# Ten of the gate and up chunks loaded in three transfers: 112, 8 and 8 partitions

## The reference

```
x = x + W_o( g_A * branch_A + g_B * branch_B + g_X * branch_X )   # gated conv, conformer conv, 4-head cross-attention
x = x + MoE(RMSNorm(x))                                          # top 4 of 32 experts
y = RMSNorm(x)
```

```
gu = xe @ w_gu[e] + b_gu[e];  gt, up = split(gu)
act = min(gt, 7) * sigmoid(1.702 * min(gt, 7)) * (clip(up, -7, 7) + 1)
out = act @ w_dn[e] + b_dn[e]      # weighted by the router's softmax gate and summed per token
```

## Time and profile before

| | |
|---|---|
| median of 3 runs | 1346.47 us (1346.32 to 1348.5) |
| the profiled execution | 1352.6 us |
| its span | 1350.5 us |
| TensorE busy | 1261.7 us, 93% |
| VectorE busy | 606.1 us, 45% |
| ScalarE busy | 207.5 us, 15% |
| GpSimd busy | 153.7 us, 11% |
| moved by DMA | 466.74 MB, mean 346 GB/s |

### The profile page before, as it was taken

One profiled execution on the slowest core, in us unless ns is written; L12 is line 12 of the kernel. 1 busy time (PEld: TensorE's weight loads), 2 busy tenths in 40 slices (PEclk: granted clock), 3 DMA queues, 4 the chain that ended last, 5 costly groups with the idle time before them and its releaser, 6 DMA issues.

```text
span 1350.5 us, 18280 instructions
## 1 busy us (share of the span) xinstructions
PE 1261.7 (93%) x7708; PEld 524.7 (39%) x7708; DVE 606.1 (45%) x1013; ACT 207.5 (15%) x305; POOL 153.7 (11%) x177
## 2 busy tenths in 40 slices
PE   7999999999999989999999999999997878787885
PEld 5756766666553222233323332333322222222221
DVE  2898322311345563434434344535444444343445
ACT  4111433210311010001000000101000111000002
POOL 2110100000012120101111111102111121111000
PEclk9999999999989999999999999999999999999898
DMA  9714716464669999999999999999999999999993
GB/s 330 261 63 135 226 63 146 167 249 161 248 261 410 424 424 426 420 428 424 423 425 394 424 407 424 423 425 420 426 421 424 424 423 424 421 424 423 422 425 141
DMA packets 91229, 466.74 MB, mean 346 GB/s; under 512 B 41952, under 2 KB 44540, under 8 KB 66263
## 3 DMA queue, kind: packets, MB, share of 16 engines
q1 hardware_dynamic: 83489, 456.74, 83.3%
q0 software_dynamic: 6240, 5.37, 1.2%
q10 hardware_dynamic: 1374, 2.76, 0.6%
HBM read 472.06 MB, written 4.26 MB: 353 GB/s over the span
## 4 chain that ended last, share of the span: by engine, by line
PE 74%; DMA 23%; DVE 2%; issue 1%; SPq 0%; ACT 0%; DVEq 0%
PE PS L1757 26%; PE PS L1379 16%; PE PS L1787 14%; DMA ring<-in_w_gu 8%; DMA arena<-in_w_gu 8%; PE PS L1819 6%; DMA ring<-in_w_dn 5%; PE PS L1559 4%; DMA arena<-in_w_dn 3%; PE PS L1603 3%; PE PS L1415 2%; PE PS L1319 1%; PE PS L1646 1%; PE PS L1506 0%; DVE XX L1275 0%
## 5 line engine op out<-in xcount | busy, mean ns | idle before, releaser
L1757 PE MATMUL PS<-ring,arena 128*32 128x512 f32 x3408 | 388.8, 605 | 37.1 <-DMA ring<-in_w_gu 19.9
L1757 PEld LDWEIGHTS PS<-ring,arena 128*32 128x32 f32 x3408 | 108.4, 111 | 308.6 <-issue 300.4
L1379 PE MATMUL PS<-arena,ring 128*128 128x320 f32 x768 | 215.2, 436 | 0.1
L1787 PE MATMUL PS<-ring,arena 128*64 128x512 f32 x880 | 198.2, 600 | 14.3 <-DMA ring<-in_w_dn 14.3
L525 POOL DMA_INDIRECT arena<-h_rows,arena x120 | 129.9, 1083 | 710.6 <-DVE arena L1202 645.5
L1379 PEld LDWEIGHTS PS<-arena,ring 128*128 128x128 f32 x768 | 145.0, 191 | 59.6 <-issue 3.2
L1236 DVE TENSOR_TENSOR arena<-PS,XX 128x1024 f32<-128x1024 f32 x32 | 39.2, 1225 | 251.5 <-PE PS L1757 203.9
L795 ACT ACTIVATE arena<-arena 128x1024 f32<-128x1024 f32 x32 | 33.8, 1058 | 716.0 <-DVE arena L1241 716.0
L1757 PE MATMUL PS<-arena 128*32 128x512 f32 x1136 | 128.7, 594 | 8.6 <-DMA arena<-in_w_gu 6.5
L1787 PEld LDWEIGHTS PS<-ring,arena 128*64 128x64 f32 x880 | 62.2, 137 | 148.6 <-issue 148.5
L1172 DVE TENSOR_TENSOR XX<-PS,XX 128x1024 f32<-128x1024 f32 x32 | 39.2, 1224 | 155.5 <-PE PS L1819 155.5
(11 more groups left out here) (210 smaller groups left out, 754.3 us busy)
## 6 DMA issues: line engine op xcount, KB each, us to landing
ring<-in_w_gu SPq DMA_DIRECT2D x96, 2048.0 KB, 25.7
ring<-in_w_dn SPq DMA_DIRECT2D x46, 2048.0 KB, 24.4
arena<-in_w_gu SPq DMA_DIRECT2D x31, 2048.0 KB, 27.5
arena<-in_w_dn SPq DMA_DIRECT2D x17, 2048.0 KB, 30.4
ring<-in_w_in SPq DMA_DIRECT2D x11, 2048.0 KB, 11.1
ring<-in_w_mem_kv SPq DMA_DIRECT2D x2, 2048.0 KB, 20.9
ring<-in_cache_mem_k SPq DMA_DIRECT2D x32, 128.0 KB, 3.3
ring<-in_cache_mem_v SPq DMA_DIRECT2D x4, 1024.0 KB, 6.2
```

What stands on the lines that cost most here:

```text
L1379: last = mm(PS[:, j % 2, 0:T], w[:, k, m * P:(m + 1) * P], hT[:, k, :], start=k == 0, stop=k == KT - 1)
L1757: last = mm(PS[32 * q:32 * q + 32, 2 * i + b, :].rearrange("p (g n) -> p g n", g=2), xT[:, k, at:at + PART], w[:, :, q, :], start=k == 0, ...
L1787: last = mm(PS[64 * h:64 * h + 64, 4 + b, :], actT[:, 4 * c + j, b * BLK:(b + 1) * BLK], moe_ring(AT[(e, 4 + c)], 4)[:, j, h * 512:(h + 1) ...
```

## The change

Of the gate and up chunks, those with number 1 of the experts 2, 5, 8, ... 29 (ten chunks) are loaded by three transfers instead of one: partitions 0 to 111, 112 to 119 and 120 to 127. All three count on the semaphore of the same place, so it rises by 48 instead of 16, and `moe_arrived` counts transfers instead of chunks. The bytes, their places and the order of everything else stay as they are.

```diff
+def transfers(m):
+
+    e, c = STREAM[m]
+    return 3 if c == 1 and e % 3 == 2 else 1
+
+
@@ moe_arrived @@
-    turns = PLACE.count(s)
-    return 16 * (mixer + turns * v + PLACE[:TURN[m]].count(s) + 1)
+    there = [transfers(n) for n in RINGED if moe_slot(n) == s]
+    here = sum(transfers(n) for n in RINGED[:TURN[m] + 1] if moe_slot(n) == s)
+    return 16 * (mixer + sum(there) * v + here)
@@ expert_chunk @@
             e, c = STREAM[m]
+            if transfers(m) == 3:
+                for rows in (slice(0, P - 16), slice(P - 16, P - 8)):
+                    sp.dma_start(moe_ring(m, 2)[rows], wgu[e, rows, 2 * c:2 * c + 2, :]).then_inc(moe_loaded(m), 16)
+                return sp.dma_start(moe_ring(m, 2)[P - 8:P], wgu[e, P - 8:P, 2 * c:2 * c + 2, :])
             if c < 4:
                 return sp.dma_start(moe_ring(m, 2), wgu[e, :, 2 * c:2 * c + 2, :])
```

## The result

| | before | after |
|---|---|---|
| median of 5 runs each, on the same chip | 1346.47 us | 1475.1 us |
| span of the profiled execution | 1350.5 us | 1472.5 us |
| TensorE busy | 1261.7 us | 1283.3 us |

The ratio is 1.0961 (95% interval 1.0939 to 1.0982). The ten changed chunks cost 128.6 us, 12.9 us each, where 2.3 us each were forecast; the time lies far outside the range.

A forecast was written before the change was run, and what follows sets the result against it. TensorE bounds the kernel until about 1000 us, then the expert-weight stream. Collisions of 37 us less 14 us give +23 us on the early half (late half +19), so 1346.5 + 23 = 1369.5 us, range 1341 to 1391.

The forecast's parts named there:

- Issues and waits at nothing: On SyncE, twenty more issues of 0.33 to 0.42 us hide behind some 25 us of backlog, no wait added: 0.
- Rows 8: Profile rows of the two final stores: 128 partitions at 401 GB/s, 64 at 229, read as paths tied to partitions.
- collisions outweigh the balance: In the weight stream, engines sharing paths cost more than shifting load between halves saves: net +23 us, chance 0.65.
- Rival 1: In the weight stream, balancing works: no collisions, small transfers use the early engines; -4.3 us, 1342.2 us, chance 0.22.
- rivals 2 and 3: Late half takes the small transfers without collisions, 1352.7 us, chance 0.07; or landing hides behind other work, 1346.5 us, chance 0.06.
- 3.7 us more for a changed chunk on the eight engines: Changed chunk, engines of the small transfers: 4.3 us, two times 1.85, misfit 0.6, less 4.95; 37 us over ten.
- 14 us credit: Early half of the engines: 9 us lead at the stream's end plus 5 us idle in two dips, set against 37 us.
- misfit of the 112 rows 0.6 (between 0 and 0.9): In each changed chunk, the 112-row transfer does not fit engines to paths one to one: 0.6 us.
- Engines that have drifted apart collide less: In changed chunks, drift lowers collisions: two small transfers at 1.85 us each, where two paths without drift gave 2.5 each.
- The two small transfers, 5.0 us in all without drift: In each changed chunk, two eight-row transfers over two paths, four rows after each other, 2.5 us each.
- the far end that was named: All eight engines on one path, no drift, in all ten chunks: 10.3 us a chunk, 1435 us, chance less than 0.05.
- The signs named beforehand: Stream from 410 us: share near 1.0, GB/s down 3 to 4%, TensorE waits before 1000 us, idle +20 us, plateau shrinks.

The follow-up runs named there:

- experiment 2: The same ten chunks as three transfers over all 128 partitions, cut by columns, against the kernel before: 1348.23 us against 1345.96, ratio 1.0007.
- experiment 10: Transfers alone, no compute, source rows and destination partitions set apart: six eight-row transfers took 15.8 us into partitions 0-7, 7.5 us into every fourth of 0-31.
- experiment 9: Only two chunks near the end changed, as rows 32-95 plus eight transfers of every fourth row, against the kernel before: 1367.85 us against 1346.91, ratio 1.0143.
- experiment 1: Transfers alone, no compute, different partition ranges: four chunks of 128 rows 21.8 us, of 112 rows 28.6 us; nine chunks with one in three transfers 53.2 us against 46.3.
- experiment 8: Transfers alone, 16 chunks, one as 112+8+8 after 0 to 4 transfers holding eight engines back: +7.2, 8.4, 10.1, 11.6, 10.9 us over plain.
- experiment 3: The ten chunks as two transfers of 112 and 16 partitions, against the kernel before: 1465.76 us, ratio 1.088.
- experiment 12: Ten extra eight-row DRAM-to-DRAM transfers ahead of expert 26, its second chunk as 112, 8 and 8 rows, against the kernel before: 1368.43 us, ratio 1.0149.

## Why the prediction was wrong, point by point

- What bounds the kernel, and that the stream's rate is what counts: right. Most of the time came out of slow DMA at a share of 1.0; some 17 us are engines that stood idle because TensorE had fallen behind, which the prediction did not have.
- Issues and waits at nothing: right (experiment 2).
- Rows 8 read as paths that belong to partitions: right, and now shown by destination (experiment 10). That collisions outweigh the balance: right in sign. Rival 1 found no gain even with other cuts (experiment 9), rivals 2 and 3 are excluded by the size.
- **The step that failed** is the price of a changed chunk, "3.7 us more for a changed chunk on the eight engines", with a 14 us credit against it. It measured 12.9 us, not confined to eight engines and without the credit. The next four points take its parts.
- The term "misfit of the 112 rows 0.6 (between 0 and 0.9)" counted the rows per path, which are nearly even, and not who writes where at what moment. Alone the misfit is 6.5 - 4.3 = 2.2 us (2.6 us at the 266 GB/s of experiment 10). That is 1.6 to 2 us of the 9.2 us a chunk that were missing. The sentence that the usual transfer "fits engines and paths one to one" was there, but its consequence was drawn for the small transfers alone. That with 112 rows no engine has a path of its own is the likely reason, but it rests on the deal in blocks that experiment 1 argues and does not show.
- "Engines that have drifted apart collide less" has the wrong sign where it was tested. In step a changed chunk costs 7.2 us, after the full lead 10.9 us (experiment 8), and in the kernel with 112 + 16 the loss grows from 7.0 to 15.5 us along the stream (experiment 3). That this drift is what the kernel's price consists of is not shown: experiment 12 took the lead away and the price stayed.
- The lead of 9 us and the idle 5 us as a credit of 14 us: not there to be had. The half that is behind is slowed as well and ends 106 us later, where the forecast had given it 19 us.
- The two small transfers, 5.0 us in all without drift, were sized well: a chunk in three parts alone is 11.5 us, less 28.6 / 4 = 7.1 us for the 112 rows, 4.3 us. In the kernel they are the smaller matter: 112 + 16 costs 12.0 us and 64 + 64 costs 12.5 us without them, against 12.9 us. Alone and in step they are not (3.8 us for 112 + 16, 7.2 us for 112 + 8 + 8).

How the missing 106 us divide: 3.7 us a chunk was forecast; in step it is 7.2 (+35 us over ten chunks), in the kernel 12.9 (+57 us more), and the credit of 14 us falls away. The 12.9 us are the measured time over ten, so that these add up confirms nothing; they only show that the largest part is the 57 us, and its cause is the one that stays open. The range ended at 1391 us because its high end kept the misfit at 0.9 us and took "no drift" as the worst case; the far end that was named, one path and 10.3 us a chunk, was also too low.

The signs named beforehand held in kind, not in size: the share stays at 1.0 while GB/s falls where changed chunks pass, though the mean over the stream falls by some 11% and not 3 to 4%; TensorE waits before 1000 us (41.68 of 50 us busy at 600 to 650 us, where it was never idle), and its waits for chunks in `ring` alone grow by 26.5 us after 1000 us (46.4 against 19.9); the plateau shrank to 2 us.

## What to carry to other kernels

Load a tile across all 128 partitions in one transfer, and cut it by columns if it has to be cut: three column cuts cost nothing measurable here, while leaving out even eight partitions halved the rate. A misfit transfer slows the plain ones in flight with it, so price it as a loss of rate for the whole stream and not as more work for the engines that it names. No way of shifting work between DMA engines by such cuts gained anything here. A share of busy engines near 1.0 says nothing of their rate; read it beside GB/s.

## What the runs showed that was not expected

- 64 partitions can be as fast per byte as 128: 32-95 at 430 GB/s, 0-63 at 206.
- 120 partitions run at 202 GB/s, 112 at 281, 128 at 428: the rate is not monotone in the count.
- The same cut costs between 3.8 and 9.1 us (112 + 16) with transfers alone, depending only on how the engines stand to each other when it comes.
